# Two decoder blocks on one core: the normalised activations h moved by 64 bytes within the partition

## The chip, the core and the metric

The kernel runs on one NeuronCore of a Trainium2 chip. Its engines are TensorE (PE; its weight loads are listed apart as PEld), VectorE (DVE), ScalarE (ACT), GpSimd (POOL) and SyncE (SP), which here starts the transfers. The metric is the device time of one launch, in microseconds (us), lower is better.

## The reference, cut to what matters

Two blocks of a language model work one after the other on 256 tokens of width 1024, all in fp32. What counts for this case are the projections: each takes normalised activations h (256 x 1024) times a weight matrix that is read once from HBM.

```
# block one
proj = rmsnorm(x, g_mix_pre) @ w_in            # 1024 x 3080: q, k, v of two attentions, forget gates
x = x + rmsnorm(y @ w_out, g_mix_post)
q, k, v = h @ w_mq, mem_n @ w_mk, mem_n @ w_mv # cross attention to 256 memory tokens
x = x + rmsnorm(o @ w_mo, g_mem_post)
x = x + rmsnorm(square(relu(h @ w_ff1)) @ w_ff2, g_ff_post)     # 1024 -> 4096 -> 1024
# block two
proj = rms_norm(x, g) @ w_in_2                 # 1024 x 8280: delta rule, sparse attention, gates
x = x + merged @ w_out_2
x = x + square(relu(h2 @ w_mlp_up)) @ w_mlp_down                # 1024 -> 4096 -> 1024
```

## The kernel before

**Split products.** TensorE gets fp32r operands. Each fp32 operand is split into a part `hi` and the rest `lo`, and a product is made of three matmuls: hi*hi, hi*lo and lo*hi. The activations h stand transposed (128 features per chunk in the partitions, 8 chunks, 256 tokens each) in `h_hi` and `h_lo`, 8192 bytes per partition each, and are written anew for each projection. `m_hi` and `m_lo` are the same for the memory tokens, `hid_hi` and `hid_lo` hold the 4096 wide hidden layer.

**Weights.** A planner cuts all weight matrices into units of 1 MB (128 partitions x 2048 floats). SyncE loads unit after unit into four slots `w_raw`; ScalarE writes the `hi` part into one of three slots `w_hi` (L399), VectorE the `lo` part over the raw one, `w_lo` (L405).

**Two forms of a unit.** In form A (lines 455 to 457, and in other orders 495 to 497 and 520 to 522) the activations are the stationary operand, 128 columns that a weight load puts into the array, and 512 columns of weights stream past. In form B (lines 467 to 469) 128 columns of weights are stationary and 256 tokens of activations stream past:

```
# form A
pe.matmul(o, hi[:, k, ts], wh[:, cs], start=q["first"] and kk == 0, stop=False)
pe.matmul(o, hi[:, k, ts], wl[:, cs], start=False, stop=False)
i = pe.matmul(o, lo[:, k, ts], wh[:, cs], start=False, stop=q["last"] and kk == 3)
# form B
pe.matmul(o, wh[:, cs], hi[:, k, :], start=k == 0, stop=False)
pe.matmul(o, wh[:, cs], lo[:, k, :], start=False, stop=False)
i = pe.matmul(o, wl[:, cs], hi[:, k, :], start=False, stop=k == KC - 1)
```

The second argument is the stationary operand, the third the streaming one; the profile names the streaming one first (`acc<-s_h_hi,s_w_hi` is form B). There are four forms of use: h in form B (parts of w_in, w_mq, w_ff1, w_in_2, w_mlp_up), h in form A (the rest of them), m in both (w_mk, w_mv), and hid in form A only (w_ff2, w_mlp_down). Two narrow products (`narrow_mm`, lines 412 to 414) take h as the streaming operand and 8 or 88 columns of weights out of `ws_hi` and `ws_lo` as the stationary one.

**Order.** The order of the work is written out by hand for each engine. Around the attentions, parts of a unit stand between the steps of the attention so that TensorE has something to do while the softmax runs elsewhere.

**Addresses.** The tiles lie one behind the other in the partition, in the order in which they are declared. In bytes from the start of a partition:

| tile | start | start modulo 128 | modulo 256 |
|---|---|---|---|
| w_lo0 to w_lo3 (over w_raw) | 16512, then every 8192 | 0 | 128 |
| w_hi0 to w_hi2 | 49280, then every 8192 | 0 | 128 |
| h_hi, h_lo | 73856, 82048 | 0 | 128 |
| x, xn, cst | 90240, 98432, 106624 | 0 | 128 |
| ws_hi, ws_lo | 123136, 126208 | 0 | 0 |
| hid_hi, hid_lo | 144960, 177728 | 64 | 64 |
| m_hi, m_lo | 209472, 217664 | 64 | 64 |

A chunk of h, m or hid is 1024 bytes, the weights of a form B matmul 512 bytes, and those of a form A matmul 2048 bytes, so that the distance of a matmul's two operands modulo 512 is that of the tiles' starts. Only in `ws_hi` and `ws_lo` is a chunk 384 bytes long.

Of the kernel before, what the change touches and what calls it, by code (L numbers as in the profile page):

```python
# [12 lines left out]
P = 128  # L13
# [175 lines left out]
def build_program(nc, w, consts, small, rel, out):  # L189
# [3 lines left out]
    with ctx:  # L193
        def sb(name, shape, dt=F32, at=ctx):
            return at.enter_context(nc.sbuf_tensor("s_" + name, shape, dt))
# [7 lines left out]
        r0.close()  # L203
        w_lo = [sb(f"w_lo{i}", [P, 2048], F32R) for i in range(RAW_SLOTS)]
        w_hi = [sb(f"w_hi{i}", [P, 2048], F32R) for i in range(SPLIT_SLOTS)]
        h_hi = sb("h_hi", [P, KC, S], F32R)
        h_lo = sb("h_lo", [P, KC, S], F32R)
        x = sb("x", [P, NT, D])
        xn = sb("xn", [P, NT, D])
        cst = sb("cst", [P, N_CONST])  # L210
# [2533 lines left out]
```

How the kernel before makes its waits and increments, by code:

```python
    def wait(self, eng, sem, k=1):  # L183
        key = (id(eng), id(sem))
        self.seen[key] = self.seen.get(key, 0) + k
        eng.wait_ge(sem, self.seen[key])
# [202 lines left out]
        def unit_hi(act, u, q=None):  # L389
            if u == 0 and q == 0:
                act.wait_ge(w_first, 16)
            if u == 0 and q == 2:
                act.wait_ge(w_loaded[0], 16)
            if u and not q:
                act.wait_ge(w_loaded[u % RAW_SLOTS], 16 * (u // RAW_SLOTS + 1))
                if u >= SPLIT_SLOTS:
                    act.wait_ge(unit_done, u - SPLIT_SLOTS + 1)
            cs = slice(0, 2048) if q is None else slice(q * 512, (q + 1) * 512)
            act.activation(w_hi[u % SPLIT_SLOTS][:, cs], w_raw[u % RAW_SLOTS][:, cs], ACT.Copy).then_inc(
                w_hi_done, 4 if q is None else 1)
# [1 line left out]
        def unit_lo(dve, u, q=None):  # L402
            dve.wait_ge(w_hi_done, 4 * u + (4 if q is None else q + 1))
            cs = slice(0, 2048) if q is None else slice(q * 512, (q + 1) * 512)
            dve.tensor_tensor(w_lo[u % RAW_SLOTS][:, cs], w_raw[u % RAW_SLOTS][:, cs], w_hi[u % SPLIT_SLOTS][:, cs].bitcast(F32),
                              ALU.subtract).then_inc(w_lo_done, 4 if q is None else 1)
# [24 lines left out]
            def chunk_ready(k):  # L431
                if fresh is not None:
                    pe.wait_ge(nt_lo, fresh + k + 1)
# [69 lines left out]
        def banks_free(pe, u):  # L503
            for b, n in zip(units[u]["banks"], units[u]["before"]):
                if n:
                    pe.wait_ge(acc_free[b], n)
```

## Time and profile before

| | |
|---|---|
| median of 3 runs | 921.78 us (921.72 to 922.14) |
| the profiled execution | span 920.1 us |
| TensorE busy | 897.4 us, 98% of the span, 5672 matmuls |
| VectorE busy | 575.2 us, 63% |
| ScalarE busy | 511.8 us, 56% |
| GpSimd busy | 89.6 us, 10% |
| read from HBM | 148 MB, 164 GB/s over the span |

The span reaches from the first to the last instruction of the profiled execution. A matmul's duration in the trace reaches to its modelled end, long after the next one has started; what a matmul costs is the time from its start to the next start.

### The profile page before, as it was taken

Reading aid. Unit: us, or ns where it says so; the run is one execution under the profiler, and the core shown is the slowest. Engines: PE = TensorE matmul, PEld = TensorE weight load, DVE = VectorE, ACT = ScalarE, POOL = GpSimd, SP = SyncE. Lnnn points to the kernel's source line nnn. Section 1 sums busy time; section 2 is a strip of 40 time slices with the busy share of each in tenths; the row PEclk is TensorE's granted clock in tenths of the full one; section 3 lists DMA queues with packets and bytes.
Section 4 is the critical chain, followed back from the end, with each engine's and each line's share of the span. In section 5 each row is a group of like instructions: output and inputs, shape, how many; then the busy total and the mean of one; then the engine's idle time right before and its main releaser. Section 6 shows DMA issues by size and latency. Waiting matters only on the chain.

```text
span 920.1 us, 14611 instructions
## 1 busy us (share of the span) xinstructions
PE 897.4 (98%) x5672; PEld 797.0 (87%) x5672; DVE 575.2 (63%) x899; ACT 511.8 (56%) x932; POOL 89.6 (10%) x111
## 2 busy tenths in 40 slices
PE   6999999999999999999999999999999999999998
PEld 6998977888899998887778989988899799998886
DVE  5455656664676664445656998889846676665333
ACT  4466666664665554335557668787255465554330
POOL 0010000000000000001000412241152101000000
PEclk9999999999999999999999999999999999999999
DMA  9756333464455566555364544454430456555552
GB/s 341 254 183 230 107 124 108 148 226 92 146 175 184 183 207 185 195 202 195 107 214 138 184 139 141 134 164 157 99 143 1 131 190 184 184 183 183 184 189 84
DMA packets 110395, 152.22 MB, mean 165 GB/s; under 512 B 6752, under 2 KB 68344, under 8 KB 109944
## 3 DMA queue, kind: packets, MB, share of 16 engines
q1 hardware_dynamic: 110328, 151.31, 50.7%
q8 instruction: 45, 0.74, 0.3%
q14 instruction: 22, 0.18, 0.1%
HBM read 147.99 MB, written 3.30 MB: 164 GB/s over the span
## 4 chain that ended last, share of the span: by engine, by line
issue 48%; PE 34%; DVE 9%; ACT 4%; POOL 2%; DVEq 1%; DMA 1%; POOLq 1%; ACTq 0%; SPq 0%
PE acc L455 4%; PE acc L469 4%; PE acc L467 4%; PE acc L468 4%; PE acc L457 4%; PE acc L456 4%; DVE s_w_lo L405 3%; ACT s_w_hi L399 1%; PE acc L495 1%; DVE s_qkvT L1522 1%; PE acc L497 1%; PE acc L496 1%; DMA s_w_raw<-in_w_out 1%; ACT s_relu_i L1445 1%; POOL s_rstd L636 1%
## 5 line engine op out<-in xcount | busy, mean ns | idle before, releaser
L405 DVE TENSOR_TENSOR s_w_lo<-s_w_raw,s_w_hi 128x2048 fp32r<-128x2048 f32 (+1 forms) x198 | 312.2, 1594 | 176.5 <-ACT s_w_hi L399 176.2
L399 ACT ACTIVATE s_w_hi<-s_w_raw 128x2048 fp32r<-128x2048 f32 (+1 forms) x198 | 262.7, 1345 | 148.6 <-PE acc L457 102.3
L467 PE MATMUL acc<-s_h_hi,s_w_hi 128*128 128x256 f32 x800 | 229.1, 286 | 0.8 <-DVE s_h_lo L690 0.8
L469 PE MATMUL acc<-s_h_hi,s_w_lo 128*128 128x256 f32 x800 | 227.3, 284 | 0.0
L468 PE MATMUL acc<-s_h_lo,s_w_hi 128*128 128x256 f32 x800 | 227.3, 284 | 0.0
L467 PEld LDWEIGHTS acc<-s_h_hi,s_w_hi 128*128 128x128 f32 x800 | 154.5, 193 | 1.6 <-issue 1.2
L468 PEld LDWEIGHTS acc<-s_h_lo,s_w_hi 128*128 128x128 f32 x800 | 154.6, 193 | 0.3
L469 PEld LDWEIGHTS acc<-s_h_hi,s_w_lo 128*128 128x128 f32 x800 | 154.4, 193 | 0.0
L457 PE MATMUL acc<-s_w_hi,s_hid_lo 128*128 128x512 f32 x224 | 88.3, 394 | 0.0
L456 PE MATMUL acc<-s_w_lo,s_hid_hi 128*128 128x512 f32 x224 | 87.8, 392 | 0.0
L455 PE MATMUL acc<-s_w_hi,s_hid_hi 128*128 128x512 f32 x224 | 86.9, 388 | 0.0
L455 PE MATMUL acc<-s_w_hi,s_h_hi 128*128 128x512 f32 x176 | 70.7, 402 | 0.8 <-DVE s_w_lo L405 0.7
L457 PE MATMUL acc<-s_w_hi,s_h_lo 128*128 128x512 f32 x176 | 68.7, 390 | 0.0
L456 PE MATMUL acc<-s_w_lo,s_h_hi 128*128 128x512 f32 x176 | 68.6, 390 | 0.0
L1082 ACT ACTIVATE s_hid_r<-acc 128x512 f32<-128x512 f32 x32 | 19.2, 600 | 69.5 <-PE acc L469 62.4
L456 PEld LDWEIGHTS acc<-s_w_lo,s_hid_hi 128*128 128x128 f32 x224 | 42.0, 188 | 9.8
L455 PEld LDWEIGHTS acc<-s_w_hi,s_hid_hi 128*128 128x128 f32 x224 | 42.1, 188 | 9.3
L457 PEld LDWEIGHTS acc<-s_w_hi,s_hid_lo 128*128 128x128 f32 x224 | 42.1, 188 | 8.3
L1509 POOL TENSOR_TENSOR s_qkvT<-s_qkvT,s_cprod 128x255 f32<-128x255 f32 (+2 forms) x36 | 29.4, 817 | 133.1 <-ACT s_cprod L1498 129.7
L455 PEld LDWEIGHTS acc<-s_w_hi,s_h_hi 128*128 128x128 f32 x176 | 33.0, 188 | 9.6 <-issue 2.4
L495 PE MATMUL acc<-s_w_hi,s_h_hi 128*128 128x512 f32 x96 | 38.7, 403 | 2.4 <-DVE s_h_lo L715 2.3
L457 PEld LDWEIGHTS acc<-s_w_hi,s_h_lo 128*128 128x128 f32 x176 | 33.0, 188 | 7.2
(323 smaller groups left out, 1429.1 us busy)
## 6 DMA issues: line engine op xcount, KB each, us to landing
s_w_raw<-in_w_in SPq DMA_DIRECT2D x43, 1024.0 KB, 5.2
s_w_raw<-in_w_ff SPq DMA_DIRECT2D x32, 1024.0 KB, 5.2
s_w_raw<-in_w_mlp_up SPq DMA_DIRECT2D x16, 1024.0 KB, 5.5
s_w_raw<-in_w_mlp_down SPq DMA_DIRECT2D x16, 1024.0 KB, 5.0
s_w_raw<-in_w_out SPq DMA_DIRECT2D x8, 1024.0 KB, 5.1
s_w_raw<-in_w_mk SPq DMA_DIRECT2D x4, 1024.0 KB, 5.4
s_w_raw<-in_w_mv SPq DMA_DIRECT2D x4, 1024.0 KB, 5.0
s_w_raw<-in_w_mq SPq DMA_DIRECT2D x4, 1024.0 KB, 5.0
```

Of the source, the lines that this page charges most:

```text
L399: act.activation(w_hi[u % SPLIT_SLOTS][:, cs], w_raw[u % RAW_SLOTS][:, cs], ACT.Copy).then_inc(w_hi_done, 4 if q is None else 1)
L405: dve.tensor_tensor(w_lo[u % RAW_SLOTS][:, cs], w_raw[u % RAW_SLOTS][:, cs], w_hi[u % SPLIT_SLOTS][:, cs].bitcast(F32), ALU.subtract).then ...
L455: pe.matmul(o, hi[:, k, ts], wh[:, cs], start=q["first"] and kk == 0, stop=False)
L456: pe.matmul(o, hi[:, k, ts], wl[:, cs], start=False, stop=False)
L457: i = pe.matmul(o, lo[:, k, ts], wh[:, cs], start=False, stop=q["last"] and kk == 3)
L467: pe.matmul(o, wh[:, cs], hi[:, k, :], start=k == 0, stop=False)
L468: pe.matmul(o, wh[:, cs], lo[:, k, :], start=False, stop=False)
L469: i = pe.matmul(o, wl[:, cs], hi[:, k, :], start=False, stop=k == KC - 1)
L495: pe.matmul(o, hi[:, k, ts], wh[:, cs], start=r["first"] and kk == 0, stop=False)
L496: pe.matmul(o, hi[:, k, ts], wl[:, cs], start=False, stop=False)
L1082: act.activation(hid_r[:, j % 2, :], hid_bank(tag, j)[:], ACT.Relu).then_inc(relu_done, 1)
L1509: i = pool.tensor_tensor(qkvT[:, c, d:S], qkvT[:, c, d:S], cprod[:, j % 2, tap, 0:S - d], ALU.add)
```

## The change

Sixteen floats that nothing uses are declared ahead of `h_hi`, and sixteen behind `h_lo`. `h_hi` and `h_lo` then start at 73920 and 82112, 64 bytes later: 64 modulo 128, and 192 modulo 256. Every tile that is declared behind them starts 128 bytes later, which leaves it where it was modulo 128. The weight slots stay where they are. No instruction is added, removed or moved, and no operand's shape changes.

```
         r0.close()
         w_lo = [sb(f"w_lo{i}", [P, 2048], F32R) for i in range(RAW_SLOTS)]
         w_hi = [sb(f"w_hi{i}", [P, 2048], F32R) for i in range(SPLIT_SLOTS)]
+        sb("before_h", [P, 16])
         h_hi = sb("h_hi", [P, KC, S], F32R)
         h_lo = sb("h_lo", [P, KC, S], F32R)
+        sb("behind_h", [P, 16])
         x = sb("x", [P, NT, D])
```

## Rows read from the trace of the kernel before

**Rows 1.** The page: TensorE's busy time, and its granted clock in 40 slices.

```profile
PE 897.4 (98%) x5672; PEld 797.0 (87%) x5672; DVE 575.2 (63%) x899; ACT 511.8 (56%) x932; POOL 89.6 (10%) x111
...
PEclk9999999999999999999999999999999999999999
```

**Rows 2.** Groups of instructions, shapes apart: count | busy, mean ns | idle before.

```profile
L467 PE MATMUL acc<-s_h_hi,s_w_hi 128*128 128x256 f32 x800 | 229.1, 286 | 0.8 <-DVE s_h_lo L690 0.8
...
L455 PE MATMUL acc<-s_w_hi,s_hid_hi 128*128 128x512 f32 x224 | 86.9, 388 | 0.0
...
L455 PE MATMUL acc<-s_w_hi,s_h_hi 128*128 128x512 f32 x176 | 70.7, 402 | 0.8 <-DVE s_w_lo L405 0.7
...
L495 PE MATMUL acc<-s_w_hi,s_h_hi 128*128 128x512 f32 x96 | 38.7, 403 | 2.4 <-DVE s_h_lo L715 2.3
...
L520 PE MATMUL acc<-s_w_hi,s_h_hi 128*128 128x512 f32 x64 | 26.2, 410 | 1.1 <-DVE s_h_lo L542 0.7 <-DVE s_h_lo L746 0.4
```

**Rows 3.** Timeline of PE, form B on h: start us, duration us; 24 matmuls apart.

```profile
299.99 0.28 PE L467 MATMUL acc<-s_h_hi,s_w_hi 128*128 128x256 f32 x1
...
302.87 0.28 PE L467 MATMUL acc<-s_h_hi,s_w_hi 128*128 128x256 f32 x1
```

**Rows 4.** Timeline of PE, form B on m; 18 matmuls apart.

```profile
99.24 0.28 PE L467 MATMUL acc<-s_m_hi,s_w_hi 128*128 128x256 f32 x1
...
101.28 0.28 PE L467 MATMUL acc<-s_m_hi,s_w_hi 128*128 128x256 f32 x1
```

**Rows 5.** Timeline of PE, form A on h; 9 matmuls apart.

```profile
652.27 0.39 PE L455 MATMUL acc<-s_w_hi,s_h_hi 128*128 128x512 f32 x1
...
654.31 0.39 PE L455 MATMUL acc<-s_w_hi,s_h_hi 128*128 128x512 f32 x1
```

**Rows 6.** Timeline of PE, form A on hid; 12 matmuls apart.

```profile
379.97 0.39 PE L455 MATMUL acc<-s_w_hi,s_hid_hi 128*128 128x512 f32 x1
...
382.72 0.39 PE L455 MATMUL acc<-s_w_hi,s_hid_hi 128*128 128x512 f32 x1
```

**Rows 7.** Timeline of PE, the narrow product of 8 columns: 24 matmuls up to 39.90.

```profile
37.15 0.28 PE L412 MATMUL aux<-s_h_hi,s_ws_hi 128*8 128x256 f32 x1
37.26 0.28 PE L413 MATMUL aux<-s_h_lo,s_ws_hi 128*8 128x256 f32 x1
...
37.49 0.28 PE L412 MATMUL aux<-s_h_hi,s_ws_hi 128*8 128x256 f32 x1
37.61 0.28 PE L413 MATMUL aux<-s_h_lo,s_ws_hi 128*8 128x256 f32 x1
...
39.90 0.40 PE L455 MATMUL acc<-s_w_hi,s_h_hi 128*128 128x512 f32 x1
```

**Rows 8.** Timeline of PE, the narrow product of 88 columns: 24 matmuls.

```profile
449.02 0.28 PE L412 MATMUL aux<-s_h_hi,s_ws_hi 128*88 128x256 f32 x1
...
451.84 0.40 PE L455 MATMUL acc<-s_w_hi,s_h_hi 128*128 128x512 f32 x1
```

**Rows 9.** Line 467 alone, by stretch: us, PE busy (count), PEclk, DMA share, GB/s.

```profile
11.00:38.00 27.00, 19.39 (x64) 1.00 0.97 352
...
262.00:346.00 84.00, 63.47 (x224) 1.00 0.60 194
493.00:606.00 113.00, 55.27 (x192) 1.00 0.48 150
747.00:829.00 82.00, 63.47 (x224) 1.00 0.60 191
```

**Rows 10.** Timelines of DVE and PE: the last unit of the first stage.

```profile
28.77 2.29 DVE L405 TENSOR_TENSOR s_w_lo<-s_w_raw,s_w_hi 128x2048 fp32r<-128x2048 f32 x1 [4.49 <-ACT s_w_hi L399]
...
31.39 0.28 PE L467 MATMUL acc<-s_h_hi,s_w_hi 128*128 128x256 f32 x1
```

**Rows 11.** The chain that ended last, by line, from 494 to 542 us and from 542 to 606 us.

```profile
by line: DVE s_w_lo L405 24.1%; ACT s_relu_i L1445 12.1%; DVE s_qkvT L1522 9.8%; issue 9.5%; ACT s_w_hi L399 7.9%; DVE s_rope_t L1319 4.8%; ACT s_cprod L1498 4.6%; DVE s_junk L1415 4.3%; DVEq L1413 3.4%; DVE s_top L1412 3.1%; DVE s_zg L1560
...
by line: PE acc L467 15.7%; PE acc L469 15.7%; PE acc L468 15.7%; DVE s_w_lo L405 9.8%; PE aux L828 7.0%; PE aux L775 6.8%; DVE s_qkvT L1522 5.4%; PE aux L809 4.5%; DVE s_qkvT L1535 3.8%; issue 3.7%; ACT s_w_hi L399 3.0%; DVEq L1521 1.5%; A
```

More of the change, by code:

```diff
@@ L205, in build_program @@
         w_hi = [sb(f"w_hi{i}", [P, 2048], F32R) for i in range(SPLIT_SLOTS)]
+        sb("before_h", [P, 16])
         h_hi = sb("h_hi", [P, KC, S], F32R)
         h_lo = sb("h_lo", [P, KC, S], F32R)
+        sb("behind_h", [P, 16])
         x = sb("x", [P, NT, D])
```

## The prediction, made before the changed kernel had run

> **What bounds the kernel now.** I read the page first. TensorE is busy 98% of the span, and its granted clock stands at 9 (90% or more) in every slice [rows 1]: it works on the higher of its two levels (2.4 GHz), and nothing is to be had from the clock. The reader should see that no other engine is near it, so a change that touches no instruction can only matter through how long one takes. The page's durations don't tell that: a form B matmul is listed with 286 ns [rows 2], but 24 of them start within 302.87 - 299.99 = 2.88 us [rows 3], 120.0 ns from start to start. So the second view is TensorE's timeline, read as distances of starts.
>
> The third view is the same timeline where the other operand is not h. Form B on m, same shapes, same slots of weights: 18 matmuls in 101.28 - 99.24 = 2.04 us, 113.3 ns [rows 4]. Form A on h takes 2.04 us for 9, 226.7 ns [rows 5]; form A on hid 2.75 us for 12, 229.2 ns [rows 6]. Nothing waits in any of these stretches. What differs is the address: h starts at 0 modulo 128 like the weights, m and hid at 64 (the table of addresses). Form B is 6.7 ns faster at the distance 64, form A 2.5 ns slower.
>
> **That the load of the next stationary operand is involved.** The narrow products stream h as form B does, but load fewer columns: 8 columns take (39.90 - 37.15) / 24 = 114.6 ns [rows 7], 88 columns (451.84 - 449.02) / 24 = 117.5 ns [rows 8], 128 columns 120.0 ns [rows 3]. The more is loaded beside a stream, the slower the stream. And low address bits count, with all tiles in one region of the memory: in the narrow product a chunk of weights is 384 bytes and one of h 1024, so the distance changes by 128 modulo 256 from chunk to chunk, and the first matmul of a chunk takes 0.11 us at 37.15 and 0.12 us at 37.49 [rows 7].
>
> The Trainium skill says the opposite ("TensorE: Matmul & The Clock Gate", Part 2, step-by-step): TensorE has two independent read ports, and loading the next weights takes no read bandwidth from the running matmul. By that rule the address could not matter and the sum would be nought, 921.8 us; rows 3, 7 and 8 speak against it, rows 4 and 5 give the sum below.
>
> **The change, part by part.**
> *No instruction* is added, removed or moved, and no wait. The 32 floats are never read: nothing.
>
> *h in form B.* Line 467 does 800 of these matmuls [rows 2], and lines 468 and 469 as many each: 2400. The trace has no h at 64, so the price is bounded. The fast bound is m's cadence, 113.3 ns, 6.7 ns less [rows 4]. On the slow side the nearest row is form A at this distance modulo 128, which is 2.5 ns worse than at 0 [rows 5, 6]. I take m's cadence: same shapes, same form, same distance modulo 128. What of it reaches the end goes by stage. Line 467's counts times three are the matmuls [rows 9]; 96 of its 800 lie outside the four stretches shown, 64 in cq and ck (4 units of 16) and 32 in mq (2 units).
> - Feed-forward, 262 to 346 and 747 to 829 us: 224 x 3 = 672 each, back to back on TensorE. 1344 x 6.7 ns = 9.0 us, all of it.
> - First stage, 11 to 38 us: 192 matmuls, 1.3 us. But the DMA queues are at 0.97 of their time there [rows 9], and the fourth unit's lo part is ready at 28.77 + 2.29 = 31.06 us, while TensorE comes to it at 31.39 [rows 10]. It can come 0.33 us earlier and no more. Behind that, 48 matmuls give 0.3 us. Together 0.65 us; the rest turns into a wait for weights.
> - cq and ck: 192 matmuls, 1.3 us, all of it. mq: 96 matmuls, 0.6 us, half of it counted (0.3), as the attention that they are laid between has a chain of its own.
> - Second block, 493 to 606 us: 192 x 3 = 576 matmuls. From 494 to 542 the chain runs over ScalarE and VectorE, and TensorE has no share among its first lines [rows 11]; a third of the matmuls (4 of the 12 units qkv) lies there and gives nothing. From 542 to 606 TensorE's lines hold 15.7 x 3 + 7.0 + 6.8 + 4.5 = 65% of the chain: 384 x 6.7 ns x 0.65 = 1.7 us.
>
> Sum of form B: 9.0 + 0.65 + 1.3 + 0.3 + 1.7 = 12.9 us less. If all of it counted it would be 2400 x 6.7 ns = 16.0 us; with the feed-forwards, cq and ck and the first stage alone, 11.0 us.
>
> *h in form A.* 176 + 96 + 64 = 336 per kind of product [rows 2], 1008 matmuls. At the distance 64 the row is hid's: + 2.5 ns, 2.5 us at most. A seventh of it lies where ScalarE and VectorE hold the chain; I take + 2.1 us. Bounds: 0 if hid's cadence is its own, + 2.5 us.
>
> *hid, m and all other tiles* move by 128 bytes and keep their place modulo 128. At nought, if 128 is the period. If the period is 256, the sign of the distance changes for them, and it is a rival.
>
> *Writers of h.* ScalarE and VectorE write 64 bytes further; no row has the same write at both places in the same stage, and these engines have idle time beside them. At nought.
>
> **The sum** is made against the profiled execution: 920.1 us of span and 1.7 us around it are the median of 921.8. 921.8 - 12.9 + 2.1 = **911.0 us**.
>
> **The rivals.**
> - *Nothing happens: 921.8 us.* m and hid could be different because they lie high in the partition (144960 and up), not because of 64 bytes. For it: no tile below that start is at 64 and streamed as fp32r. Against it: the narrow product, where 128 bytes of distance make 0.11 or 0.12 us within one region [rows 7]. This is also where the rule of the Trainium skill named above would put the time.
> - *The sign counts, and it turns out slower: 930 us.* In form B the stationary operand now lies 64 bytes below the streaming one (modulo 128 the same as m, modulo 256 the other side of m's +64); m in form B has it on the other side, and form A on hid has exactly this side, and is the slow one. If form B on h takes hid's penalty, 2400 x 2.5 ns = + 6.0 us, and form A another 2.5 us, the time is 921.8 + 8.5 = 930.3 us. Its place is every unit of form B; it decides as soon as form B's cadence is above 120.0 ns. For it: the two sides have been seen in different forms only. Against it: form B is the form in which 64 helped.
> - *The sign counts, and both forms swap: 915 us.* Form B loses 2.5 ns (+ 6.0 us, and m with 192 matmuls from 113.3 to 122.5, + 1.8 us), but form A on h and on hid gets the good side and falls to what m's cadence gives for 256 columns more, 113.3 + 106.7 = 220.0 ns (106.7 ns is 256 columns at 2.4 GHz; rows 5 less rows 4 give 113.4). That is 1008 x 6.7 = 6.7 us and about 864 x 9.2 = 7.9 us less. 921.8 + 7.8 - 14.6 = 915.0 us.
> - *The gain is real, but is given back: 918 us.* If TensorE's weights come late in the feed-forward too. Against it: DMA stands at 0.60 there [rows 9].
>
> **How the numbers follow.** The likeliest case (m's cadence for form B, hid's for form A) has 0.65; its own range is 906 to 914 us: 905.8 if all 16.0 us count and form A costs nothing, 914 if the second block and mq give nothing, the feed-forward nine tenths (8.1 us) and form A costs 2.5 us: 921.8 - 8.1 - 0.65 - 1.3 + 2.5 = 914.3. The swap has 0.08, the gain given back 0.05, nothing 0.12, the slower case 0.10. The range leaves out the slower case and a tail: 905.5 to 922 us. A measurement of this kernel tells about 0.2% (1.8 us) from no change. Faster by more: 0.65 + 0.08 + 0.05 = 0.78; within it: 0.12; slower: 0.10.
>
> **What the profile of the changed kernel would show.** Form B on h 113.3 ns from start to start in the feed-forward, where it was 120.0 [rows 3]; form A on h at 229, where it was 226.7 [rows 5]; hid still 229.2 [rows 6] and m 113.3 [rows 4]. The stage from 262 to 346 us is 4.5 us shorter, that from 747 on as well. In the first stage TensorE waits for line 405 before the fourth unit. From 494 to 542 us nothing is shorter. The prediction is wrong if h keeps 120.0 ns (place, not distance), if it goes above (the side counts), or if hid and m change their cadence, which would mean that 128 bytes are not a period.

## The result, and the profile after

The changed kernel takes 925.78 us in the median of 6 runs (924.18 to 926.39), the kernel before 921.96 us (921.72 to 922.69). The ratio is 1.0036, with a 95% interval of 1.0026 to 1.0047: slower by 0.4%, where 911.0 us and a chance of 0.78 for faster were forecast. The profiled execution has a span of 922.8 us, 2.7 us more than before, with the clock granted in full as in [rows 1].

The timeline of TensorE in the changed kernel, with the same stretches as in [rows 3] to [rows 6] (start us, duration us; all lines are two higher, as two lines were added). Form B on h, 24 matmuls apart:

```profile
299.97 0.28 PE L469 MATMUL acc<-s_h_hi,s_w_hi 128*128 128x256 f32 x1
...
302.80 0.28 PE L469 MATMUL acc<-s_h_hi,s_w_hi 128*128 128x256 f32 x1
```

Form B on m, 18 apart, first in the stretch that [rows 4] shows (a stretch is a row of matmuls of one kind with no other kind between them), then in the next one:

```profile
99.53 0.28 PE L469 MATMUL acc<-s_m_hi,s_w_hi 128*128 128x256 f32 x1
...
101.57 0.28 PE L469 MATMUL acc<-s_m_hi,s_w_hi 128*128 128x256 f32 x1
...
103.51 0.28 PE L469 MATMUL acc<-s_m_hi,s_w_hi 128*128 128x256 f32 x1
...
105.63 0.28 PE L469 MATMUL acc<-s_m_hi,s_w_hi 128*128 128x256 f32 x1
```

Form A on h, 12 apart, and form A on hid, 12 apart:

```profile
653.12 0.39 PE L457 MATMUL acc<-s_w_hi,s_h_hi 128*128 128x512 f32 x1
...
655.92 0.39 PE L457 MATMUL acc<-s_w_hi,s_h_hi 128*128 128x512 f32 x1
```

```profile
379.85 0.39 PE L457 MATMUL acc<-s_w_hi,s_hid_hi 128*128 128x512 f32 x1
...
382.65 0.39 PE L457 MATMUL acc<-s_w_hi,s_hid_hi 128*128 128x512 f32 x1
```

Form B on h fell from 120.0 ns [rows 3] to 2.83 / 24 = 117.9, a third of what was expected. Form A on h rose from 226.7 [rows 5] to 2.80 / 12 = 233.3. And two things moved that were to stay: hid in form A from 229.2 [rows 6] to 233.3, and m in form B from 113.3 to 2.12 / 18 = 117.8, in eight of its nine stretches. The ninth is that of [rows 4], and it still takes 2.04 / 18 = 113.3. Of the 24 stretches of form B on h, one of 24 matmuls ran at 113.3, all others at 117.8. So form B shows two cadences here although every operand stands at one place; the experiments come back to this.

Summed over each trace, from every matmul's start to the next start:

| matmuls | before, mean ns | after, mean ns | change of the sum |
|---|---|---|---|
| form B on h, 2400 | 119.9 | 117.7 | - 5.9 us |
| form A on h, 1008 | 228.2 | 233.3 | + 4.4 us |
| form A on hid, 767 | 228.9 | 233.3 | + 3.3 us |
| form B on m, 192 | 113.8 | 117.2 | + 0.6 us |
| form A on m, 96 | 230.1 | 233.6 | + 0.3 us |

(The means leave out distances above 135 and 250 ns, at which something was waited for or the form changed; the sums hold all.) Together + 2.7 us, the whole change of the span; all other matmuls together changed by 0.0. The cadences alone, over the matmuls that the means hold, make - 5.2, + 4.8, + 3.4, + 0.6 and + 0.3 us, + 3.9 in all; 1.2 us less went into the distances that are left out.

### The profile page after: what moved, and what is told of

Same layout as the page of the kernel before. It is cut to its first block, busy times and chain, and to the rows that moved or that the text cites. A ratio compares the mean times of both kernels' runs of the same rounds, so it can differ in the third digit from the quotient of the medians.

```text
span 922.8 us, 14611 instructions
## 1 busy us (share of the span) xinstructions
PE 900.5 (98%) x5672; PEld 791.1 (86%) x5672; DVE 575.0 (62%) x899; ACT 512.0 (55%) x932; POOL 89.7 (10%) x111
## 4 chain that ended last, share of the span: by engine, by line
issue 47%; PE 38%; DVE 7%; ACT 4%; POOL 2%; DVEq 1%; POOLq 1%; DMA 0%; ACTq 0%
PE acc L457 5%; PE acc L459 5%; PE acc L458 5%; PE acc L470 4%; PE acc L469 4%; PE acc L471 4%; DVE s_w_lo L407 2%; ACT s_w_hi L401 1%; PE acc L497 1%; PE acc L498 1%; PE acc L499 1%; DVE s_qkvT L1524 1%; PE aux L1820 1%; PE aux L1687 1%; ACT s_relu_i L1447 1%
## 5 line engine op out<-in xcount | busy, mean ns | idle before, releaser
L469 PE MATMUL acc<-s_h_hi,s_w_hi 128*128 128x256 f32 x800 | 225.9, 282 | 1.7 <-DVE s_h_lo L692 1.7
L470 PE MATMUL acc<-s_h_lo,s_w_hi 128*128 128x256 f32 x800 | 224.5, 281 | 0.0
L471 PE MATMUL acc<-s_h_hi,s_w_lo 128*128 128x256 f32 x800 | 224.0, 280 | 0.0
L469 PEld LDWEIGHTS acc<-s_h_hi,s_w_hi 128*128 128x128 f32 x800 | 151.1, 189 | 2.5 <-issue 2.1
L470 PEld LDWEIGHTS acc<-s_h_lo,s_w_hi 128*128 128x128 f32 x800 | 151.1, 189 | 0.3
L471 PEld LDWEIGHTS acc<-s_h_hi,s_w_lo 128*128 128x128 f32 x800 | 150.5, 188 | 0.0
```

## The experiments

In what follows a distance is the place of h, hid or m minus that of the weight slots, modulo 256 bytes. Before the change h had the distance 0 and hid and m had 192 (64 - 128). After it, **all three have 64**. The weight slots themselves stand at 128 modulo 256 (the table of addresses).

**One part alone: only the tiles behind h move, by 128 bytes.**

```
+        sb("behind_h", [P, 32])      # nothing ahead of h_hi
```

> Only the tiles behind h move, by 128 bytes; h stays at the weights' own place modulo 256. Theory 1 (the pair of places modulo 256 sets a matmul's cadence, each operand pair for itself): form B on h 120.0 ns and form A on h 226.7 ns as before the change; hid at 233.3, m in form B at 117.3, as after the change; about 3.3 + 0.6 + 0.3 us above the kernel before, 925.5 to 926. Theory 2 (the padding acts on the kernel as a whole, say by the place of h itself or of what the other engines read, and hid and m follow h): hid and m are back at 229.2 and 113.3, and the time is 922.

926.86 us, ratio 1.0053 (1.0038 to 1.0068). The timeline, form B on h 24 apart and form A on hid 12 apart:

```profile
299.99 0.28 PE L468 MATMUL acc<-s_h_hi,s_w_hi 128*128 128x256 f32 x1
...
302.87 0.28 PE L468 MATMUL acc<-s_h_hi,s_w_hi 128*128 128x256 f32 x1
...
379.65 0.40 PE L456 MATMUL acc<-s_w_hi,s_hid_hi 128*128 128x512 f32 x1
...
382.45 0.40 PE L456 MATMUL acc<-s_w_hi,s_hid_hi 128*128 128x512 f32 x1
```

h keeps 120.0 ns, hid has 233.3: theory 1. The price of the floats behind h is all of the loss and more. So 128 is not a period. Two things are not as expected. m in form B held 113.3 in three of its nine stretches and 117.8 in six, all at the distance 64. And the time is 0.9 us above the expected range; the trace has 1.0 us more between the starts of matmuls that are neither form A nor form B, which no run explains.

**The other part alone: only h moves, by 64 bytes.**

```
+        sb("before_h", [P, 16])
+        sb("behind_h", [P, 48])
```

> Only h moves, by 64 bytes; the tiles behind it move by 256 bytes. Theory 1: form B on h 117.7 ns, form A on h 233.3 as after the change; hid 229.2 and m 113.3 as before it; 5.9 us less and 4.4 us more of TensorE's time, so 920.5 to 922.5. Theory 2: hid and m as after the change, 925 to 926. If the period is longer than 256, hid and m show new numbers here.

920.90 us, ratio 0.9986 (0.9976 to 0.9995). Form B on h 24 apart, once early and once later, and hid 12 apart:

```profile
16.15 0.28 PE L469 MATMUL acc<-s_h_hi,s_w_hi 128*128 128x256 f32 x1
...
18.87 0.28 PE L469 MATMUL acc<-s_h_hi,s_w_hi 128*128 128x256 f32 x1
...
299.89 0.28 PE L469 MATMUL acc<-s_h_hi,s_w_hi 128*128 128x256 f32 x1
...
302.71 0.28 PE L469 MATMUL acc<-s_h_hi,s_w_hi 128*128 128x256 f32 x1
...
379.77 0.39 PE L457 MATMUL acc<-s_w_hi,s_hid_hi 128*128 128x512 f32 x1
...
382.52 0.39 PE L457 MATMUL acc<-s_w_hi,s_hid_hi 128*128 128x512 f32 x1
```

117.5 ns and 229.2 ns. The early rows give 2.72 / 24 = 113.3: at the distance 64 h, too, can run at m's old cadence. It did so up to a pause near 24 us (262 ns between two starts), and held 117.8 behind it. With hid and m back at the distance 192 modulo 256 their cadences are back too; h alone is worth 1.3 us less than before.

**h at the distance 192.**

```
+        sb("before_h", [P, 48])
+        sb("behind_h", [P, 16])
```

> h moves by 192 bytes, the tiles behind it by 256. Theory 1 with signed distances: in form B the streaming h then has the side of the weights that m had before, 113.3 ns; in form A h has the side that hid had before, 229.2 ns; hid and m unchanged. This is the case that the prediction took the change for: 16 us less of TensorE's time in form B, 2 more in form A, 910 to 912 us. If only being off the weights' place by an odd 64 bytes counts (side without meaning), form B on h stays at 117.7 and form A at 233.3, 921 to 922.

918.57 us, ratio 0.9961 (0.9951 to 0.9972), a spread of 917.32 to 920.68. Neither expectation. In the profiled run, of 24 stretches of form B on h 16 ran mainly near 113.5 ns and 8 near 117.8, and the two of 624 matmuls were among the slow ones. 24 matmuls in one of these two, and in a fast stretch:

```profile
299.80 0.28 PE L469 MATMUL acc<-s_h_hi,s_w_hi 128*128 128x256 f32 x1
...
302.63 0.28 PE L469 MATMUL acc<-s_h_hi,s_w_hi 128*128 128x256 f32 x1
...
493.10 0.28 PE L469 MATMUL acc<-s_h_hi,s_w_hi 128*128 128x256 f32 x1
...
495.82 0.28 PE L469 MATMUL acc<-s_h_hi,s_w_hi 128*128 128x256 f32 x1
```

2.83 / 24 = 117.9 ns and 2.72 / 24 = 113.3. Between two pauses (distances above 135 ns) the cadence did not change once the first matmuls were past; the first stage had 113.3 before a pause of 0.9 us and 117.8 behind it. hid, which stood at the distance 192 as before, was at 233.3 this time. One program, one distance, two cadences.

**h at the distance 128.**

```
+        sb("before_h", [P, 32])
+        sb("behind_h", [P, 32])
```

> h moves by 128 bytes, the tiles behind it by 256. Theory 1: a new distance, no row has it; the narrow product of 8 columns was fastest at this distance, so form B at 113 to 118 and form A at 220 to 233, 905 to 925 us. If the period is 128, form B 120.0, form A 226.7 and 922 us.

922.53 us, ratio 1.0007 (0.9998 to 1.0016). Form B on h took 118.7 ns on average (2.85 us for 24), a little above the expected 113 to 118, form A 232.6, hid 228.9. The distance 128 is not the distance 0 (119.9 and 228.2); in the sum it comes to the same time.

**The matmuls by themselves, over the distances.** The pattern of forms A and B, repeated with nothing else running; `off` is the distance, and the output is a copy of x.

```
k, m = c % 8, c // 8 % 2
st = w_[a][:, k * 256 + m * 128:k * 256 + m * 128 + cols]
mv = h_[b][:, off + k * 256:off + k * 256 + 256]
pe.matmul(ps[n % 2][0:cols, 0:256], st, mv, start=first, stop=last)
```

> Nothing of the reference is computed: after a warm-up, TensorE only repeats the three-matmul pattern of form B (96 and then 48 matmuls) and form A (48 and 48) with h at 0, 32, 64 and so on bytes from the weights' place, up to 448, then 16 and 48; the output is a copy of x. Each h distance begins with a pause; the last two stretches of it run on without one. Theory 1 (the distance modulo 256 alone sets the cadence, and the load of the next operand is what disturbs the stream): form B 120.0 ns at 0 and 256, 117.7 at 64 and 320, 113.3 at 192 and 448; form A 226.7, 233.3 and 229.2 there; the same with and without the pause. Theory 3 (at an odd 64 bytes there are two steady rhythms, and how a stretch starts picks one): 64, 192, 320 and 448 show either 113.3 or 117.8 in form B and 229.2 or 233.3 in form A, not always the same one with and without the pause. Rival: the cadences come from the other engines' traffic in the full kernel; then all distances agree here, near 109 to 113 ns, as nothing else runs.

Its timeline merges equal matmuls, so that a row is a stretch of 48 without a pause ahead: form B and form A at the distances 0, 64 and 192.

```profile
64.56 5.92 PE L77 MATMUL ps<-s_h,s_w 128*128 128x256 f32 x48
70.32 11.07 PE L83 MATMUL ps<-s_w,s_h 128*128 128x512 f32 x48
...
145.70 5.82 PE L77 MATMUL ps<-s_h,s_w 128*128 128x256 f32 x48
151.36 11.37 PE L83 MATMUL ps<-s_w,s_h 128*128 128x512 f32 x48
...
308.41 5.62 PE L77 MATMUL ps<-s_h,s_w 128*128 128x256 f32 x48
313.87 11.15 PE L83 MATMUL ps<-s_w,s_h 128*128 128x512 f32 x48
```

The first takes (70.32 - 64.56) / 48 = 120.0 ns a matmul, the third 5.66 / 48 = 117.9, the fifth 5.46 / 48 = 113.8 with its first few, which are slower. The steady cadence (mean of the last 30 distances of a stretch, with a pause / without one):

| distance | form B, ns | form A, ns |
|---|---|---|
| 0 and 256 | 120.0 / 120.0 | 226.7 / 226.7 |
| 16 | 116.7 / 116.7 | 233.3 / 233.3 |
| 32 | 117.8 / 116.7 | 233.3 / 233.3 |
| 48 | 118.4 / 118.3 | 233.3 / 233.3 |
| 64 and 320 | 117.8 / 117.8 | 233.3 / 233.3 |
| 96 | 120.0 / 120.0 | 234.2 / 234.3 |
| 128 | 118.7 / 120.0 | 233.3 / 232.2 |
| 160 | 117.3 / 118.7 | 233.3 / 233.3 |
| 192 and 448 | 113.3 / 113.3 | 228.9 / 228.9 |
| 224 | 118.4 / 118.3 | 233.3 / 233.4 |

The usual numbers of the full kernel come back with no other engine at work, so the cadences of 120.0, 117.8, 113.3 and 226.7 to 233.3 ns need no other engine. Each cell is one stretch of one execution; the 113.3 that the kernel also showed at 64 did not come up here. 256 is a period (256, 320 and 448 repeat 0, 64 and 192). 64 and 192 are not alike. Theory 3 was not shown here: 192 always held 113.3 in form B. At 32, 128 and 160 the two stretches of form B differ, 116.7 and 117.8 at 32 for instance.

**h at 192, hid and m at the weights' own place.**

```
+        sb("before_h", [P, 48])
+        sb("behind_h", [P, 32])
```

> h moves by 192 bytes, the tiles behind it by 320, so that hid and m lie at the weights' own place modulo 128 and 256. By theory 1 and 3 alike hid falls into the one rhythm of that place, 226.7 ns in form A (hid was 229.2 before and 233.3 in the run with h at 192), m in form B 120.0, h as in the run with h at 192. Against that run 768 x 6.7 ns = 5.1 us less and 192 x 6.7 = 1.3 more: 914 to 916 us. If hid's cadence comes from something other than its place, it stays at 233.3 and the time is 918.6 or above.

912.27 us (909.96 to 913.35), ratio 0.9888 (0.9873 to 0.9903). The profiled run was the 909.96 us one, the fastest of four. Form B on h 24 apart, hid 12 apart:

```profile
299.73 0.28 PE L469 MATMUL acc<-s_h_hi,s_w_hi 128*128 128x256 f32 x1
...
302.45 0.28 PE L469 MATMUL acc<-s_h_hi,s_w_hi 128*128 128x256 f32 x1
...
379.98 0.39 PE L457 MATMUL acc<-s_w_hi,s_hid_hi 128*128 128x512 f32 x1
...
382.70 0.39 PE L457 MATMUL acc<-s_w_hi,s_hid_hi 128*128 128x512 f32 x1
```

113.3 and 226.7 ns. Here the two stretches of 624 held 113.3 throughout, which is 2 x 624 x 4.4 ns = 5.5 us against the run with h at 192, and hid was 2 x 384 x 6.6 ns = 5.1 us faster. The gain in the medians, 6.3 us, is more than the 5.1 that hid was expected to give, and the time is below the expected 914 to 916. The rhythm of the two long stretches would explain that. h stands where it stood in the run with h at 192, and no run shows why they took the faster rhythm here.

**h_hi alone moves, h_lo keeps its place modulo 256.**

```
+        sb("before_h", [P, 16])
         h_hi = sb("h_hi", [P, KC, S], F32R)
+        sb("between_h", [P, 48])
         h_lo = sb("h_lo", [P, KC, S], F32R)
```

> Half of the change: h_hi moves by 64 bytes, h_lo by 256 and so keeps its place modulo 256, as do the tiles behind. If each matmul's cadence is set by its own pair of places, form B shows 120.0 ns where h_lo streams (line 468 as the kernel before numbers it) and 117.7 where h_hi does, 118.4 on average; form A likewise between 226.7 and 233.3, 231. If a stretch has one common rhythm, all three products show the same cadence, or one that neither place alone has. Time 920 to 923 us either way; hid 229.2 and m 113.3.

924.47 us, ratio 1.0022 (1.0013 to 1.0032). In the first long stretch the matmul that streams h_lo took 122.1 ns (116 and 128 in turn), the two that stream h_hi 117.5 and 117.1: h_lo, at the distance 0, did not have the 120.0 of that distance. A matmul's cadence is therefore not its own pair's alone; its neighbours count. hid, again at 192, ran at 233.3 in both its stretches where 229.2 was expected. That is 3.3 us, and it covers the time above the expected 920 to 923. m kept 113.9.

**Load, place, width of the point, two rhythms.** The same bare matmuls, with the number of loaded columns, the weights' own place and what stands ahead of a stretch varied.

```
for e in (0, 64, 192):                  # distance
    for cols in (8, 32, 64, 96, 128):   # columns loaded
        STRETCHES += [("B", e, 96, cols, 0, True)]
for wo in (64, 128, 192):               # weights and h moved together
    for e in (0, 64, 192):
        STRETCHES += [("B", e, 96, 128, wo, True)]
```

> Again nothing of the reference is computed, only matmuls in the pattern of form B (and A), the output being a copy of x. Four questions. (1) Is it the load? With 8, 32, 64, 96 and 128 columns loaded at the distances 0, 64 and 192: if the load of the next operand disturbs the stream, all three distances agree near 113.3 ns with 8 columns and part with more, to 120.0, 117.8 and 113.3; if the streamed tile's own place does it, they differ by as much with 8 columns as with 128. (2) Does the distance count or the place? Weights and h moved together by 64, 128 and 192 bytes: distance gives 120.0, 117.8 and 113.3 again for 0, 64 and 192; place gives other numbers. (3) Is 192 a point or a plateau? 176, 184, 200 and 208 bytes: 113.3 if a plateau of 64 bytes around it, 117 or more if a point. (4) Are there two rhythms at 192? One to six single matmuls of 128 columns stand ahead of a stretch, without a pause: if how a stretch starts picks the rhythm, some of the twelve stretches hold 117.8 (form B) or 233.3 (form A); if not, all hold 113.3 and 229.

(1) Its timeline, stretches of 96: 8 and 128 columns at the distance 0, 8 and 128 at 64, 8, 64 and 128 at 192.

```profile
40.56 11.27 PE L90 MATMUL ps<-s_h,s_w 128*8 128x256 f32 x96 [0.34 <-ACT s_dummy L65]
...
87.42 11.78 PE L90 MATMUL ps<-s_h,s_w 128*128 128x256 f32 x96 [0.34 <-ACT s_dummy L65]
...
99.61 11.07 PE L90 MATMUL ps<-s_h,s_w 128*8 128x256 f32 x96 [0.35 <-ACT s_dummy L65]
...
145.92 11.58 PE L90 MATMUL ps<-s_h,s_w 128*128 128x256 f32 x96 [0.34 <-ACT s_dummy L65]
...
157.90 11.06 PE L90 MATMUL ps<-s_h,s_w 128*8 128x256 f32 x96 [0.34 <-ACT s_dummy L65]
...
180.84 11.64 PE L90 MATMUL ps<-s_h,s_w 128*64 128x256 f32 x96 [0.34 <-ACT s_dummy L65]
...
204.80 11.16 PE L90 MATMUL ps<-s_h,s_w 128*128 128x256 f32 x96 [0.35 <-ACT s_dummy L65]
```

The steady cadence:

| columns loaded | distance 0 | 64 | 192 |
|---|---|---|---|
| 8 | 115.6 | 113.3 | 113.3 |
| 32 | 117.8 | 113.3 | 113.3 |
| 64 | 113.3 | 116.6 | 119.0 |
| 96 | 116.0 | 113.3 | 117.0 |
| 128 | 120.0 | 117.8 | 113.3 |

With 8 columns the distances nearly agree (113.3 to 115.6 ns), with 128 they part (113.3 to 120.0). So the number of loaded columns counts; as fewer loaded columns also write fewer rows of the result, the load alone isn't shown by this. But "the more is loaded, the slower" is false for these stretches: at 192 the full 128 columns are as fast as 8, and 64 are the slowest.

(2) Weights and h together at 64, 128 and 192 bytes: 120.0, 117.8 and 113.3 for the distances 0, 64 and 192, but for one: the distance 192 with the weights at 128 held 117.8. Where the streamed tile stands does not decide by itself, as its cadence followed its distance from the loaded one in eight of nine stretches; this is what speaks for the load of the next operand. In the bare program the weights otherwise stand at 0 modulo 256, so the exception is the kernel's own place of the weights; with one stretch for it, place and chance can't be told apart. (3) 176, 184, 200 and 208 bytes gave 119.3, 120.0, 120.0 and 119.2: 113.3 is a point, gone at 8 bytes beside it, and neither 119.2 nor 120.0 is one of the two rhythms of 192. (4) The distance 192 twice after a pause (weights at 0 and at 128 bytes, in the rows at 204.80 above and 276.26 below), then stretches without a pause behind single matmuls: form B behind one and behind two, form A behind three and behind four:

```profile
276.26 11.58 PE L90 MATMUL ps<-s_h,s_w 128*128 128x256 f32 x96 [0.35 <-ACT s_dummy L65]
...
375.54 5.87 PE L90 MATMUL ps<-s_h,s_w 128*128 128x256 f32 x48
...
398.06 5.68 PE L90 MATMUL ps<-s_h,s_w 128*128 128x256 f32 x48
...
428.40 11.21 PE L96 MATMUL ps<-s_w,s_h 128*128 128x512 f32 x48
...
451.25 11.41 PE L96 MATMUL ps<-s_w,s_h 128*128 128x512 f32 x48
```

The first row took 11.58 us where the row at 204.80 above took 11.16, for the same matmuls. The stretch at 375.54 holds 117.8 ns to its end, that at 398.06 113.3; form A at 428.40 holds 228.9, at 451.25 233.3. So at the distance 192 there are two steady rhythms in either form. These two slow stretches are the only ones of the twelve behind single matmuls; the other ten held 113.3 and 228.9. As this is one execution, it doesn't show that the number of single matmuls decides.

**The same program as with h at 192, profiled again, on another chip.**

> The same program as the one with h moved by 192 bytes, profiled once more. Theory 3 (two rhythms at this distance, picked at the start of a stretch by small differences in time): some long stretches of form B on h, or of form A on hid, that held 117.8 or 233.3 ns in the first profile hold 113.3 or 229 in this one, or the other way round, and the time differs by about 2.8 us for each of the two long stretches (624 x 4.5 ns). If the program alone decides, each stretch shows the cadence of the first profile.

919.07 us. Timelines of the two profiles of this one program, form A on hid, 12 apart; first profile, then second:

```profile
379.64 0.40 PE L457 MATMUL acc<-s_w_hi,s_hid_hi 128*128 128x512 f32 x1
...
382.44 0.40 PE L457 MATMUL acc<-s_w_hi,s_hid_hi 128*128 128x512 f32 x1
```

```profile
379.98 0.39 PE L457 MATMUL acc<-s_w_hi,s_hid_hi 128*128 128x512 f32 x1
...
382.73 0.39 PE L457 MATMUL acc<-s_w_hi,s_hid_hi 128*128 128x512 f32 x1
```

2.80 / 12 = 233.3 ns against 2.75 / 12 = 229.2: the first hid stretch fell into the other rhythm, worth 384 x 4.4 ns = 1.7 us (the runs differ by 1.6 us). The second hid stretch and both long stretches of form B kept theirs (233.3 and 117.8), and of the shorter ones five changed, in both directions. The expectation was of a change in the 624-matmul stretches; it came in hid.

**Each tile at its own best distance.** h and m at 192, hid at 0.

```
+        sb("before_m", [P, 48], at=r1)      # beside the paddings of h at 192, hid at 0
         m_hi = sb("m_hi", [P, KC, S], F32R, at=r1)
```

> Each tile at the place that was best for it by the measured distances: h at 192 bytes from the weights' place (form B 113.3 ns), hid at 0 (form A 226.7), and now m at 192 as well, by 48 more floats ahead of m_hi. Against the run with h at 192 and hid at 0 (912.3 us) m in form B falls from 119.5 to 113.5 ns, 192 matmuls, 1.2 us, and rises by 1 to 3 ns in form A, 96 matmuls, 0.1 to 0.3 us: 911 to 912 us. If the stages with m are bound by the attention, no difference: 912.3.

912.63 us, ratio 0.9891 (0.9875 to 0.9908), no difference from 912.27. In this profile one long stretch of form B on h held 117.8 and the other 113.3, and m in form B held 117.8 in four of its seven stretches of 24 matmuls: at 192 m, too, has two rhythms. The gain of 1.2 us did not appear; in the trace form B on m took 0.6 us less than in that of the run with h at 192 and hid at 0 (23.9 against 24.4 us, pauses included), too little for the medians to tell.

## Why the prediction was wrong, point by point

- **TensorE is the bound, and only cadences matter.** Right. The granted clock stayed, the other matmuls changed by 0.0 us, and the two forms account for the span's + 2.7 us: + 3.9 by cadence, - 1.2 in the pauses between.
- **"Same shapes, same form, same distance modulo 128": wrong, and this is the step that failed.** The period is 256. The table of addresses had the column: h was moved to the distance 64, while m's 113.3 ns were measured at 192. The term of - 12.9 us for form B (- 16.0 before the shares by stage) measured - 5.9 us in TensorE's time; h at 64 runs at 117.8 in 23 of its 24 stretches, and at 117.8 without the kernel around it. The 113.3 that was counted on does occur at 64, but not often enough: in the changed kernel in one short stretch of h and in one of m. The rival of the sign was named, and given 0.10 and 0.08, because "form B is the form in which 64 helped"; it had been 192 that helped.
- **"hid, m and all other tiles keep their place modulo 128. At nought": wrong for the same reason.** They moved from 192 to 64: + 3.3 us for hid, + 0.6 and + 0.3 for m in forms B and A. Moved alone, they made the kernel 0.5% slower. At 64 hid was at 233.3 in all four long stretches of two traces, and the bare form A was too; at 192 hid was at 229 in seven of the twelve long stretches of six traces and at 233.3 in five. So 229.2 was not safe at the old place either, though the kernel before shows it in both.
- **Form A on h, + 2.1 us:** direction right, size off, for the same reason. hid's 229.2 was read at 192; at 64 form A on h runs at 233.3: + 4.4 us.
- **The rivals.** "Nothing happens" did not come. The rule of the Trainium skill ("TensorE: Matmul & The Clock Gate", Part 2, step-by-step) is that loading the next weights takes no read bandwidth from the running matmul. It would have left the time at 921.8 us, and the trace doesn't bear it out: 8 loaded columns took 115.6 ns and 128 loaded columns 120.0 at the distance 0, nothing else running, and the distance from the loaded operand changed the cadence. Whether it is read bandwidth that is lost, no run shows. The slower rival priced form B above 120.0 ns; it fell to 117.8, so its price for form B did not come. Its sign did: the kernel got slower, by form A on h and by hid.
- **"The more is loaded beside a stream, the slower."** It held for the three numbers at hand, and not as a rule.
- **Sizes by stage.** The prediction kept 0.65 of 1.3 us of the first stage and less than half of the second block's. With form B at 117.8 the gains were too small to test these shares.

**What stays open.** The changed kernel's median is 3.8 us above the one before, its profile 2.7 us; the profiled run was one of the quicker ones. Other rhythms in the other runs would explain it, but they weren't profiled. Why 128 loaded columns at 192 bytes go undisturbed, and what picks the rhythm at 64 and at 192, no run here shows. Each figure for fewer loaded columns is one stretch of one execution, so it is open whether it would come out the same again. And 2400 x 6.7 ns = 16 us of form B were never reached in full: the best profile, 909.96 us, had its long stretches at 113.3 ns, several short ones at 117.8.

## What to carry to other kernels

Measure a matmul from start to start, by pair of operands; where the same shape has two cadences in one trace and nothing waits, look at the operands' addresses, and compare them modulo every power of two that the tiles distinguish, not only the smallest that fits. Padding moves everything declared behind it: decide the place of each operand by itself (here h at 192 bytes from the weights modulo 256 and hid at 0 gave 1.1%), and test each part of a shift alone. Prefer a distance with one steady rhythm, as 0 was in every long stretch seen (120.0 and 226.7 ns), where a distance with a faster one may or may not lock into it.

## What the runs showed of the hardware that was not expected

- A stream of fp32r matmuls with a load of 128 columns in between has a cadence that depends on the two operands' distance modulo 256 bytes: 113.3 to 120.0 ns for 256 streamed columns, 226.7 to 234.3 ns for 512, and the best point is gone 8 bytes to either side (113.3 at 192; 120.0 at 184 and 200, one stretch each).
- The two forms don't want the same distance: 192 is best with 256 streamed columns, 0 with 512.
- At one distance there can be two steady rhythms: 113.3 and 117.8 ns at 64 (mostly 117.8) and at 192 (mostly 113.3), and 229 and 233.3 ns at 192. Once its first matmuls are past, a stretch keeps its rhythm for up to 624 matmuls; it changed only behind a pause. The same program can take another one in another execution (hid 233.3, then 229.2 on another chip).
- The number of loaded columns acts in no simple order: at 192 bytes 113.3, 113.3, 119.0, 117.0 and 113.3 ns for 8, 32, 64, 96 and 128 columns, one stretch each.
